# Decode attention with ten key buffers a turn, keys transposed in place, and kv decode rows in column tiles

## The reference

```
kv = (rmsnorm(h, norm_kv) @ w_kv)                    # 1024 -> 6 slots x 4 kv heads x 64
new_rows = kv[:, :, :4]; k, v of branches: compressed blocks, selected blocks, window
p_c = softmax(q @ kc + bias); o_c = p_c @ vc          # 32 compressed blocks of 64 tokens
idx = top_k(forced or summed p_c, 16)                 # blocks that a query may read
p_s = softmax(q @ k_sel + bias); o_s = p_s @ v_sel    # tokens of the selected blocks
p_w = softmax(q @ k_win + bias); o_w = p_w @ v_win    # last 512 tokens
out = g0 * o_c + g1 * o_s + g2 * o_w
```

## Time and profile before

| | us |
|---|---|
| median of 3 runs | 2131.95 |
| lowest and highest | 2129.97, 2134.59 |
| profiled execution | 2129.85 |
| its span, first to last instruction | 2128.1 |
| kv projection, of the span | 636.2 to 702.9 |
| prompt attention | 783 to 905 |
| decode attention | 905.6 to 1082.9 |
| output projection and MoE | from 1082.9 |

### The profile page before, as it was taken

The page is one execution under the profiler, slowest core; times in us unless marked ns, Lnnn a source line. Parts: engine busy times, 40 slices in busy tenths (PEclk is TensorE's granted clock), DMA queues, the critical chain, the costliest instruction groups (busy, mean ns, idle before and its releaser), DMA issues.

```text
span 2128.1 us, 36327 instructions
## 1 busy us (share of the span) xinstructions
PE 1945.2 (91%) x15417; PEld 1562.4 (73%) x15417; DVE 401.2 (19%) x930; ACT 260.1 (12%) x565; POOL 138.1 (6%) x198
## 2 busy tenths in 40 slices
PE   6799998999999978786786999999999999999995
PEld 5589986777767765554566969788796959697882
DVE  3795022000010025543422000000000000000002
ACT  1000011000000114433312000000000000000001
POOL 2071001200000010023201000000000000000001
PEclk9899998999999965678897999999999999999997
DMA  9755655944734224067763979999898979798994
GB/s 243 199 161 161 206 182 175 382 139 138 277 127 111 73 89 167 1 210 254 235 160 115 295 264 343 303 297 311 284 319 277 328 266 340 263 343 304 293 312 162
DMA packets 353746, 484.68 MB, mean 228 GB/s; under 512 B 32548, under 2 KB 310062, under 8 KB 353004
## 3 DMA queue, kind: packets, MB, share of 16 engines
q1 hardware_dynamic: 325600, 392.40, 58.0%
q10 hardware_dynamic: 14924, 45.66, 6.5%
q0 software_dynamic: 13120, 45.15, 6.1%
HBM read 450.51 MB, written 40.98 MB: 231 GB/s over the span
## 4 chain that ended last, share of the span: by engine, by line
issue 46%; PE 42%; DMA 4%; DVE 3%; ACT 2%; another core or an unknown queue 1%; ACTq 1%; POOL 0%; SPq 0%; DVEq 0%; POOLq 0%
PE ps L1415 14%; PE ps L1445 7%; PE ps L1539 4%; PE ps L1561 3%; DMA arena<-in_state_win_kv 3%; PE ps L1580 2%; PE ps L1598 1%; PE ps L1644 1%; PE ps L1722 1%; PE ps L1630 1%; PE ps L1786 1%; PE ps L1383 1%; ACT arena L864 1%; PE ps L1661 1%
## 5 line engine op out<-in xcount | busy, mean ns | idle before, releaser
L1871 PEld LDWEIGHTS ps<-arena 128*128 128x128 f32 x5632 | 633.1, 192 | 5.2 <-issue 5.1
L1871 PE MATMUL ps<-arena 128*128 128x128 f32 x5632 | 633.4, 275 | 1.3 <-ACT arena L899 1.3
L1415 PE MATMUL ps<-arena 128*128 128x288 f32 x1216 | 303.8, 414 | 20.8 <-DMA arena<-in_conv_w_pw 15.7
L1881 PE MATMUL ps<-arena 128*128 128x512 f32 x704 | 304.2, 593 | 1.7 <-DVE arena L1327 1.7
L1415 PEld LDWEIGHTS ps<-arena 128*128 128x128 f32 x1216 | 235.2, 194 | 88.7 <-DMA arena<-in_conv_w_pw 14.9
L1881 PEld LDWEIGHTS ps<-arena 128*128 128x128 f32 x704 | 133.1, 190 | 168.1 <-issue 168.1
L1327 DVE TENSOR_TENSOR arena<-arena,ps 128x256 f32<-128x256 f32 x88 | 37.1, 421 | 883.1 <-ACT arena L915 883.1
L1445 PE MATMUL ps<-arena 64*64 64x128 f32 x4096 | 160.4, 313 | 5.0 <-issue 5.0
L1445 PEld LDWEIGHTS ps<-arena 64*64 64x64 f32 x4096 | 156.1, 248 | 9.0 <-issue 8.4
L1007 DVE SCALAR_TENSOR_TENSOR arena<-arena 128x256 f32<-128x256 f32 x240 | 119.9, 578 | 0.0
L915 ACT ACTIVATE arena<-ps 128x256 f32<-128x256 f32 x88 | 33.8, 384 | 531.1 <-PE ps L1871 531.0
(11 more groups left out here) (298 smaller groups left out, 1161.5 us busy)
## 6 DMA issues: line engine op xcount, KB each, us to landing
arena<-in_moe_w_gate SPq DMA_DIRECT2D x88, 1024.0 KB, 6.5
arena<-in_moe_w_up SPq DMA_DIRECT2D x88, 1024.0 KB, 7.2
arena<-in_moe_w_down SPq DMA_DIRECT2D x88, 1024.0 KB, 4.9
arena<-in_cache_kv SPq DMA_DIRECT2D x176, 256.0 KB, 5.5
arena<-in_cache_kv POOLq DMA_DIRECT2D x80, 256.0 KB, 7.1
xg_scratch<-arena POOLq DMA_DIRECT2D x26, 512.0 KB, 17.6
arena<-in_conv_w_pw SPq DMA_DIRECT2D x12, 1024.0 KB, 14.1
arena<-in_cmp_w ACTq DMA_DIRECT2D x6, 2048.0 KB, 21.8
```

Source lines behind the costliest of these rows:

```text
L1415: ins = mm(dst, w[:, k, c * P:(c + 1) * P], rhs[:, k, :], start=(k == 0), stop=(k == KD - 1))
L1871: ins = mm(dst, w[:, k, c * P:(c + 1) * P], XeT[:, k, :], start=(k == 0), stop=(k == KD - 1))
L1881: ins = mm(ps[:, 4 + c, :], He[:, 2 * k + kk, :], w[:, kk, 512 * c:512 * (c + 1)], start=(k == 0 and kk == 0), stop=(k == 10 and kk == 1))
```

## The change

- **Buffers.** `key_slot(pr, u)` gives each of the ten units of a turn its own 1024 words. Turn 0 uses the weight ring; of the later turns, units 0 and 1 lie in the queries' memory, 2 to 4 in that of the prompt's kv rows, 5 to 9 in the weight ring. Values keep their two halves.
- **Transposes in place.** ScalarE copies a unit's transposed keys back over the keys (`KTs` is gone), and the scores read them there.
- **When units are issued.** All ten of turn 0 wait for `flip_mm` alone, the start of the prompt attention, and have two semaphores of their own (`kv_first0`, `kv_first1`), of which a transpose waits for the full count. In turn 1 units 0 to 4 wait for the end of the prompt attention, 5 to 9 for scores of turn 0. Later a unit waits for the scores of the same unit a turn before (`s_unit`). The wait for `o_mm` stays.
- **Order.** The transposes of the next turn's first two units move from behind a turn's outputs to ahead of its softmax, with a wait for their copies (`kt_out`); on ScalarE these two copies move ahead of the exponentials.
- **Others.** The first two weight slots of the output projection wait for the last two scores instead of the last transposes. The ranking buffer `ahead` gets its own memory. `pg_ready` is merged into `pc_ready`.
- **kv projection.** The 32 decode rows are multiplied in four column tiles: for each of eight steps, four products of 64 columns, whose results lie in four groups of 32 partitions of one bank; ScalarE copies them with four instructions.

```diff
+        def key_slot(pr, u):
+            if pr == 0:
+                return (7 * 1024, KRING, KRING + 1024, KRING + 2048, 8 * 1024, KRING + 3072, KRING + 4096,
+                        9 * 1024, 0, 1024)[u]
+            if u < 2:
+                return QT0 + u * 1024
+            if u < 5:
+                return KV0 + (u - 2) * 1024
+            return KRING + (u - 5) * 1024
+
+        def key_sem(pr, u):
+            return f"kv_first{u % 2}" if pr == 0 else f"kv_in{u}"
...
         def kv_unit(eng, page, pr, u):
-            kt, b2, slot = u // 2, u % 2, (10 * pr + u) % 5
-            k0 = KRING + slot * 4 * KVC
+            kt, b2 = u // 2, u % 2
+            k0 = key_slot(pr, u)
...
-            if 10 * pr + u >= 5:
-                eng.wait_ge(sem("kt_tr"), 10 * pr + u - 4)
+            if pr == 0:
+                eng.wait_ge(sem("flip_mm"), 1)
+            elif pr == 1 and u < 5:
+                eng.wait_ge(sem("prompt_done"), 1)
+            elif pr == 1:
+                eng.wait_ge(sem("s_unit"), (1, 2, 2, 3, 4)[u - 5])
             else:
-                eng.wait_ge(sem("flip_mm"), 1)
-            if u < 2 and pr == 1:
-                eng.wait_ge(sem("prompt_done"), 1)
-            elif u < 2 and pr > 1:
+                eng.wait_ge(sem("s_unit"), 5 * (pr - 1) + kt + 1)
+            if u < 2 and pr > 1:
                 eng.wait_ge(sem("o_mm"), pr)
...
-            sp.wait_ge(sem("kt_tr"), 10 * PAIRS)
-            weights(START["wout"], START["wout"] + 2)
+            for j in range(2):
+                sp.wait_ge(sem("s_unit"), 5 * (PAIRS - 1) + 4 + j)
+                weights(START["wout"] + j, START["wout"] + j + 1)
...
-                sc.activation(kv[0:TSN, 2, j * KVC:(j + 1) * KVC], ps[0:TSN, bk + 2, 0:KVC], ACT.Copy)\
-                  .then_inc(sem("kv_ev"), 1)
+                for r in range(4):
+                    c0 = j * KVC + r * HD
+                    ins = sc.activation(kv[0:TSN, 2, c0:c0 + HD], ps[32 * r:32 * r + 32, bk + 2, 0:HD], ACT.Copy)
+                ins.then_inc(sem("kv_ev"), 1)
...
-                for u in range(10):
-                    g = 5 * pr + u // 2
-                    act.wait_ge(sem("kt_tr"), 10 * pr + u + 1)
-                    if g >= 2:
-                        act.wait_ge(sem("s_unit"), g - 1)
-                    bk = 2 * (u % 2)
-                    sc.activation(KTs[2 * (g % 2) + u % 2], ps[:, bk:bk + 2, :], ACT.Copy).then_inc(sem("kt_out"), 1)
+                for g in range(10 * pr + (2 if pr else 0), min(10 * pr + 12, 10 * PAIRS)):
+                    act.wait_ge(sem("kt_tr"), g + 1)
+                    bk = 2 * (g % 2)
+                    sc.activation(view(key_slot(g // 10, g % 10), 2, 512), ps[:, bk:bk + 2, :], ACT.Copy)\
+                      .then_inc(sem("kt_out"), 1)
...
-                for t, (t0, n) in enumerate(TILES):
+                for t, (t0, n) in enumerate(TILES[:2]):
                     for k in range(KD):
                         operand(k)
-                        ins = mm(ps[0:n, bk + t, 0:KVC], xnT[:, k, t0:t0 + n], w[:, k, :],
-                                 start=(k == 0), stop=(k == KD - 1))
+                        mm(ps[0:n, bk + t, 0:KVC], xnT[:, k, t0:t0 + n], w[:, k, :],
+                           start=(k == 0), stop=(k == KD - 1))
+                for k in range(KD):
+                    for r in range(4):
+                        ins = mm(ps[32 * r:32 * r + 32, bk + 2, 0:HD], xnT[:, k, TP:T], w[:, k, HD * r:HD * (r + 1)],
+                                 start=(k == 0), stop=(k == KD - 1), skip_group_check=True)
...
-                pe.wait_ge(sem(f"kv_in{u}"), (pr + 1) * (64 if kt < 4 else 32))
+                pe.wait_ge(sem(key_sem(pr, u)), 4 * 64 + 32 if pr == 0 else pr * (64 if kt < 4 else 32))
...
                 if pr < PAIRS - 1:
                     block_scores(pr + 1)
+                    ktr(pr + 1, 0)
+                    ktr(pr + 1, 1)
+                    pe.wait_ge(sem("kt_out"), 10 * pr + 12)
...
                 ins.then_inc(sem("o_mm"), 1)
-                if pr < PAIRS - 1:
-                    ktr(pr + 1, 0)
-                    ktr(pr + 1, 1)
```

More of the change, by code:

```diff
@@ L153, in build @@
         rstd = take(T)
+        KV0 = cursor[0]
         kv = take(3, 6 * KVC)
+        QT0 = cursor[0]
         QT = take(KD, T)
@@ L252, in build @@
         qtflat = QT.rearrange("p a b -> p (a b)")
-        KTs = [f[:, 2 * j * 512:2 * (j + 1) * 512].rearrange("p (a b) -> p a b", a=2)
-               for f in (qtflat, kvflat) for j in range(2)]
         Om = qtflat[:, 2048:2048 + P]
-        ahead = kvflat[:, 2048:2048 + NFREE * NFREE].rearrange("p (a b) -> p a b", a=NFREE)
         Scs = take(2, NBLK)
@@ L268, in build @@
         assert VLO + 2 * 20 * KVC <= VHI
+        ahead = view(VLO + 2 * 20 * KVC, NFREE, NFREE)
+        assert VLO + 2 * 20 * KVC + NFREE * NFREE <= VHI
         V = [view(VHI, 2, 20, KVC), view(VLO, 2, 20, KVC)]
@@ L287, in build @@
         assert top_pa <= VHI
+        def key_slot(pr, u):
[9 more added lines that the diff above has]
+            return f"kv_first{u % 2}" if pr == 0 else f"kv_in{u}"
+        assert KRING + 5 * 1024 == 7 * 1024 and 4 * KVC == 1024
         phase()
@@ L446, in kv_unit @@
                     src = a["cache_kv"][bass.ds(pg, 1), :, 2:4].rearrange("g l s k d -> (g l) s (k d)")
-                    eng.dma_start(dst, src).then_inc(sem(f"kv_in{u}"), 16)
+                    eng.dma_start(dst, src).then_inc(sem(key_sem(pr, u)), 16)
             else:
                 w = a["state_win_kv"][2 * pr + b2].rearrange("(n l) s k d -> l n s (k d)", l=P)
-                eng.dma_start(view(k0, 4, KVC), w[:, :, 0, :]).then_inc(sem(f"kv_in{u}"), 16)
-                eng.dma_start(view(v0, 4, KVC), w[:, :, 1, :]).then_inc(sem(f"kv_in{u}"), 16)
+                eng.dma_start(view(k0, 4, KVC), w[:, :, 0, :]).then_inc(sem(key_sem(pr, u)), 16)
+                eng.dma_start(view(v0, 4, KVC), w[:, :, 1, :]).then_inc(sem(key_sem(pr, u)), 16)
         block = ctx.enter_context(nc.Block())
@@ L1198, in blocks @@
                 v.tensor_scalar(Pcs, x, sm[:, 1:2], None, ALU.mult).then_inc(sem("pc_ready"), 1)
-                dve.wait_ge(sem("pc_ready"), pr + 1)
-                v.tensor_scalar(x, Pcs, gateS[:, pr, 0:1], None, ALU.mult).then_inc(sem("pg_ready"), 1)
+                dve.wait_ge(sem("pc_ready"), 2 * pr + 1)
+                v.tensor_scalar(x, Pcs, gateS[:, pr, 0:1], None, ALU.mult).then_inc(sem("pc_ready"), 1)
                 dve.wait_ge(sem("imp_mm"), pr + 1)
@@ L1707, in block_sums @@
             def block_sums(pr):
-                pe.wait_ge(sem("pc_ready"), pr + 1)
+                pe.wait_ge(sem("pc_ready"), 2 * pr + 1)
                 mm(ps[:, 6, 32:32 + NBLK], samekv, Pcs, start=True, stop=True).then_inc(sem("imp_mm"), 1)
@@ L1717, in ktr @@
                 bk = 2 * (u % 2)
-                k0 = KRING + (g % 5) * 4 * KVC
+                k0 = key_slot(pr, u)
                 for a2 in range(2):
@@ L1732, in scores @@
                 for b2, a2, r in quarters:
-                    ins = mm(ps[r, bk, :], query(pr, b2, a2), KTs[2 * (g % 2) + b2][:, a2, :], start=True,
+                    ins = mm(ps[r, bk, :], query(pr, b2, a2), view(key_slot(pr, 2 * kt + b2), 2, 512)[:, a2, :], start=True,
                              stop=not biased, skip_group_check=True)
```

2 lines of the change are left out of this document (1 added, 1 removed).

## The result

The changed kernel takes 2080.65 us, median of its runs (2075.59 to 2082.16), the kernel before 2133.27 in the same comparison (2129.97 to 2141.11). The ratio is 0.9754, with a 95% interval of 0.9731 to 0.9778: 52.6 us less. The forecast was 2081 us. The profiled execution took 2080.4 us with a span of 2078.6, 49.5 less than the span before.

| stretch | before, us | after, us | difference |
|---|---|---|---|
| up to the kv projection | 636.2 | 638.7 | +2.5 |
| kv projection | 66.7 | 53.3 | -13.4 |
| query projection to end of prompt attention | 202.7 | 202.1 | -0.6 |
| decode attention, to the end of the outputs | 174.3 | 132.2 | -42.2 |
| from there to the routing of the MoE | 68.4 | 72.1 | +3.7 |

What follows compares the result with a forecast made beforehand. The prediction took the decode attention to be bound by DMA transfers and their pause each turn. From 2129.85 us, less 40.4 and 10.8, it got 2078.7, plus 2.1 for the median: 2081 us, range 2070 to 2096.

Steps and rivals of the forecast that it cites:

- What bounds the kernel: Decode attention: a turn of 41 to 46 us is the DMA's 30.1 us, plus its pause, plus ramps.
- Turns by TensorE's pace: Decode attention: key loop, wait for exponentials, softmax and outputs sum to 32.5 us a turn; stage 40.4 us less.
- The early loads at nothing: First turn's second five units, loaded during the prompt attention, cost nothing; without empty DMA slices about 20 us.
- The move of the early transposes: Decode attention: 2.05 us a turn added before the exponentials, 2.2 us gone behind the outputs; worth about nothing.
- (c): Decode attention: TensorE's clock stays at 1.2 GHz, stage 224 us, kernel 2171 us; chance 0.04, other losses included.
- Slack of the loads: Decode attention: turn 2's first units land within 8 us of issue, 5 us before they are wanted.
- Column tiles: kv projection: decode rows take 1.6 us a weight slot, not 3.6; 10.8 us saved in all.
- columns have stopped counting: kv projection: short products in four tiles stay at 25 ns each, so a slot doesn't reach 0.93 us.
- The total: Whole kernel: 40.4 and 10.8 us less, giving 2081 us; chance of 2076 to 2088 us 0.65.
- (a): Decode attention: late loads pace the turns, costing 13 us; kernel 2094 us, chance 0.15.
- (b): kv projection: column tiles don't overlap, a slot stays at 3.6 us; kernel 2092 us, chance 0.07.
- (d): Faster: clock stays at 2.4 GHz in turn 0 and column tiles reach their lower bound; 2072 us, chance 0.08.

Runs made afterwards that it cites:

- e3: Changed kernel without the loads of values in turns 2 and 3, which reuse those of turns 0 and 1: 2074.32 us, ratio 0.9726.
- e7: Changed kernel with units 5 to 9 of the first turn issued when the prompt attention ends, not when it starts: 2092.6 us, ratio 0.9824.
- e6: Changed kernel with the next turn's first two units transposed between the probabilities' transposes and the outputs: 2076.54 us, ratio 0.9737.
- e10: Changed kernel with early transposes back behind the outputs and sixteen unread identity transposes in the freed place: 2074.88 us, ratio 0.9723.
- e5: Changed kernel with the next turn's first two units transposed behind the outputs and copied after the softmax, as before: 2084.36 us, ratio 0.9788.
- e5b: Second run of the changed kernel with the next turn's first two units transposed behind the outputs: 2084.13 us, ratio 0.9759.
- e4: Changed kernel with units of turns 2 and 3 issued three scores later, or at the turn's last score: 2098.5 us, ratio 0.9822.
- e8: Changed kernel with the two inner loops of the kv decode rows exchanged, eight products of one tile in a row: 2088.66 us, ratio 0.9792.
- e9: Changed kernel with each kv decode product of 64 columns cut into two of 32: 2078.97 us, ratio 0.9746.
- e1: Kernel before with only the column tiles for the kv decode rows: 2121.37 us, ratio 0.9942.

## Why the prediction was right, and where it wasn't

**What bounds the kernel.** Right: the pause of the DMA was a turn's surplus. It no longer holds up a turn, turn 1 is 31.6 us and not 44.8, and `e3` shows that nothing waits for data any more.

**Turns by TensorE's pace.** The sum of 15.35 + 4.75 + 6.8 + 5.6 came out within 0.6 us in each term of turn 1. 31.6, 32.9 and 30.7 us stand against 32.5, 32.5 and 30.4; the 32.9 has a gap of 1.02 in it that the sum didn't have. Turn 0 took 36.9 and not 38.5: its outputs ran at the full clock (3.70 us for the 128 instructions, 925.40 on, where the earlier trace rows has 5.33). Stage: 42.2 us less, 40.4 forecast.

**The early loads at nothing.** Right: the prompt attention is as long as before (122.0 us from 772 on, 122.6 before). `e7` prices them against loads that come late and are awaited together, 14 us.

**The move of the early transposes, "worth about nothing".** The step that failed, though its number hardly entered the total. By waits it is right: `e6`, which undoes it in another way, is 1.3 us from after over the stage, and `e10`, with the old order and the fill, 0.6. In the runs it is worth more: put back behind the outputs it costs 8 us of the stage (`e5`, `e5b`). The low clock behind the last score is seen to cost 1.3 us of that, in turn 1; the most of turns 2 and 3 is a stop for instructions and the low clock behind it, whose places the move shifts. The forecast reckoned the granted clock for the whole stage (rival (c)), took its low stretches to follow waits for transfers, and had no term for a fetch. In after no wait for a transfer is left, and the clock is still 0.50 from 951.80 to 955.21, inside the softmax; two stops for instructions, of 1.0 and 0.7 us, stand in its outputs.

**Slack of the loads.** 2.6 us and not 5 by the landing in after, 3.6 by `e4`, since the first unit took 10.5 and 9.6 us to land and not the median 8.

**Column tiles.** The mechanism was right (`e8`: without overlap three times as long), the size not. The term of 1.6 us a slot was mis-sized. It came from a row of eight instructions of 32 columns (25 ns each); 64 in a row, of 64 columns, take 16 ns each, 1.03 us, and 128 of 32 columns 9.6 (`e9`). So the row of eight doesn't show the steady rate, and "columns have stopped counting" was wrong; what else those eight pay for, no run shows apart. The rule of the Trainium skill that I set beside it ("TensorEngine Tiling (Array Packing)", Performance Considerations, about 60 cycles for each product, by estimate 25 ns at 2.4 GHz) agreed with that row and not with these: `e9` has 9.6 ns an instruction. The Trainium skill speaks there of the latency of one product, these rows show a rate. The stage gained 13.4 us, 10.8 forecast: six times 2.57, less 0.5 of ScalarE at the end and 1.2 because the first slot ran longer at a lower clock (10.0 us of full-size products, 8.8 before), which makes 13.7.

**The total.** Both parts gained more than forecast, 55.6 us against 51.2; 6 us came back in the other stretches. The change touches of these only the issue of two weight slots of the output projection, and no product there waits for a transfer. The output projection took 33.5 us and not 31.3, with a clock of 0.77 in its first 9.7 us; `e1`, whose decode attention is that of before, has 33.0 there too. Where in such a stretch the clock falls differs between executions. That the two misses cancel is luck; it makes 2081 against 2080.65 look better than its terms.

**Rivals.** (a) is refuted by `e3`, (b) by `e1`, while `e8` shows what it would have cost, (c) by the clock of 0.86 to 1.00. (d) was nearest in its second half: the tiles went almost to their lower bound of 0.93 us.

## What to carry to other kernels

Where the DMA rate by slices shows a pause once in each turn, find which buffer's release opens it again; a ring as deep as the turn's work turns a transfer-paced turn into an engine-paced one, and its length can then be added up from the timeline before it is built. Ask what the matrix engine does while others work: a place with nothing to do can cost the clock of what follows beside its own length (1.3 us in turn 1 of `e5b`, nothing in `e6`), so work that must be done anyway is best put there. Before a difference between two runs is put down to the clock, find the instruction up to which they agree, and see whether a fetch of instructions stands there. Take a rate from a long run of like instructions, not from a row of eight.

## What the runs showed of the hardware

- Products of 32 rows in four column tiles, tiles taking turns: 16.1 ns an instruction at 64 columns (after), 9.6 at 32 (`e9`); in the same tile one after the other, 49 ns at 64 (`e8`).
- With 48 transposes of an identity matrix whose results no one reads the decode attention was 8.8 us shorter (140.3 to 131.6, `e5b` to `e10`), at a granted clock of 1.00 in turns 1 and 2 and not 0.90 and 0.86. 1.3 us of it is the clock in the outputs of turn 1; 5.8 are a stop for instructions and the low clock behind it, which `e10` doesn't have.
- TensorE stops for 0.4 to 2.5 us inside runs of instructions that wait for nothing, at one or two places of an execution: beside data queues at 340 to 355 GB/s, or in turn 3 at 230 to 255. Each of 17 such stops ends 1.3 to 1.6 us after a packet of 16 KB of the instruction queue has landed. In the outputs of turn 2 there is none where the queues run at half rate (`e3`) or are nearly empty (the kernel before).
- After a wait of 6 us for a transfer, sixteen transposes take 3.68 us and not 1.95 (`e4`, after).
